# Stick-breaking heads: running sums as two short products of a high and a low part in place of one full fp32 product

## The chip, the cores and the metric

The kernel runs as one program on 1 core of one Trainium2 chip. The metric is the device time of one execution in microseconds (us); less is better. The values shown are medians over runs of the same program.

## The reference, cut to what matters

The reference is a chain of transformer blocks on 256 tokens of width 1024, all in fp32. The change touches one piece of it, the attention of heads 0 to 7 in the first layer of the second block. Each of these heads is 64 wide and is called a stick-breaking head:

```python
strict = kpos[None, :] < qpos[:, None]
z = jnp.einsum('bhqd,bhkd->bhqk', q_blk, k).astype(jnp.float32) * scale
log_keep = jnp.where(strict, jax.nn.log_sigmoid(-z), 0.0)
suffix = lax.cumsum(log_keep, axis=3, reverse=True)
between = jnp.concatenate([suffix[..., 1:], jnp.zeros_like(suffix[..., :1])], axis=-1)
weight = jnp.where(strict, jnp.exp(jax.nn.log_sigmoid(z) + between), 0.0)
return jnp.einsum('bhqk,bhkd->bhqd', weight.astype(v.dtype), v)
```

The other heads of that layer are softmax heads, and everything around them (projections, output matrix, gated feed-forward parts) is dense matrix products with weights streamed from memory.

## The kernel before, in words

**Weights.** All weight matrices are packed into 231 pieces of 128 x 2048 fp32 (1 MB each). A piece is loaded by a DMA of the sync queue into one of three `raw` buffers, ScalarE (ACT) casts it to `hi` (fp32r, the high part, L2359), VectorE (DVE) subtracts to get `lo` (raw minus hi, L2685), and TensorE (PE) then makes three fp32r products, hi*hi, hi*lo and lo*hi. There are three `hi` and three `lo` buffers, so the cast of piece i+3 waits until TensorE has used piece i.

**Order.** Every engine runs one list of instructions in order. The list, `script`, is made on the host by a planner. `emit(kind, pe=..., act=..., dve=...)` appends a step and adds its estimated costs to each engine's due time. In the attention stage `weave` runs many generators side by side: the two tracks that split weight pieces, the tracks of the query and key norms, a filler (`projections`, which makes the query, key and value products and then the product with `w_out_2`), and a pool of up to PAIRS = 4 head pairs. At each turn it takes the generator whose next engine comes free first; a generator that yields None is stuck until something else has been emitted. So a changed cost or an added step can change the order of all that follows in the stage. The parts of the first attention layer are made in the order Q1, K1, Q0, V0, K0, V1 (0 and 1 are halves of 512 columns), then `w_out_2`, whose k-th block of rows needs the output of pair k.

**A stick-breaking pair.** Pairs m = 0 to 3 are stick-breaking, two heads each (`sticks`), pairs 4 to 7 are softmax pairs (`softmaxes`), and pair m + 4 starts when pair m is over. The steps of a stick pair are: `sb_z` on TensorE (scores, L2280); `sb_log` on ScalarE (two copies out of PSUM L2611, then Abs L2614, Exp L2616, Ln L2618); `sb_keep` on VectorE (L3128, and the two triangular masks L3130 and L3131); `sb_sum` on TensorE (the running sums, L2290 to L2292); `sb_add` on VectorE (L3136); `sb_exp` on ScalarE (L2622); `sb_mask` on VectorE (L3140, L3141); then `pv`, the product with the values, on TensorE (L2328), and the split of its result (`o_hi` L2638, `o_lo` L3162). The scores of a head lie in a tile of 384 columns: 256 queries against the first 128 keys, and the last 128 queries against the last 128 keys. Softmax pairs have `soft` (L2308), `soft_top`, `soft_exp` (L2627, L2629), `soft_div`, `soft_turn` (transposes, L2317), `turn_out` (L2635) and `pv`. The query and key evacuation ahead of `sb_z` is L3050.

**The running sum before.** The tile `Eb[i]` (fp32, both heads of a pair) is the moving operand; the stationary operand is `ntri`, minus the triangle of ones, or `nones`, minus all ones, both fp32 constants. For each head there is one product of 256 columns and two of 128 columns. The `nt` buffers hold a norm's turned rows, and `fgb` is a buffer that the second attention layer uses for its forget gate.

## Time and profile before

| what | value |
|---|---|
| median of 3 runs | 1449.74 us (1448.24 to 1449.86) |
| span of the profiled execution | 1447.7 us |
| TensorE busy | 1434.0 us, 99% |
| TensorE weight loads busy | 1233.0 us, 85% |
| VectorE busy | 1013.2 us, 70% |
| ScalarE busy | 769.4 us, 53% |
| GpSimd busy | 29.4 us, 2% |

The profiled execution has no time of its own on record apart from its span, which runs from its first to its last instruction. The median of the runs is 2.0 us above that span; that is what lies around it, start and end, and the scatter of runs. Busy times overlap between engines. A matrix product appears as a weight load (PEld) and a matmul (PE); the ends of matmuls are modelled and overlap, so the distance between starts is the measure of their cost.

### The profile page before, as it was taken

The numbers are of one execution on the slowest core, as the hardware profiler recorded it, in microseconds if no ns is written. First come the engines' busy times: TensorE is split into PE (matmuls) and PEld (weight loads), VectorE is DVE, ScalarE is ACT, GpSimd is POOL, SyncE is SP. The second block draws the span as 40 slices with busy tenths as digits, with TensorE's granted clock in tenths as the row PEclk, the third lists the DMA queues.
The fourth block names the chain that finished last, engine by engine and source line by source line (L and its number), as shares of the span: only waits on it lengthen the run. The fifth ranks groups of instructions, "written<-read, shape, count | busy, mean of one in ns | idle before, by whom it ended". The sixth has DMA issues, their size and how long they took to land.

```text
span 1447.7 us, 22866 instructions
## 1 busy us (share of the span) xinstructions
PE 1434.0 (99%) x9408; PEld 1233.0 (85%) x9408; DVE 1013.2 (70%) x1341; ACT 769.4 (53%) x1047; POOL 29.4 (2%) x96
## 2 busy tenths in 40 slices
PE   9999999999999999999999999999999999999999
PEld 8988898888887888888878888888888887788887
DVE  6876567886356787548768877478774688687753
ACT  7744564654336565445665554355553556665542
POOL 0000000000001200000000000000000000000000
PEclk9999999999999999999999999999999999999999
DMA  8431235555544455544424555545555453255552
GB/s 337 169 119 63 87 117 204 198 202 203 190 159 175 156 220 179 202 174 180 170 88 157 193 199 182 201 158 205 190 189 191 152 196 123 94 207 188 190 188 87
DMA packets 36104, 249.11 MB, mean 172 GB/s; under 512 B 4129, under 2 KB 4257, under 8 KB 6689
## 3 DMA queue, kind: packets, MB, share of 16 engines
q1 hardware_dynamic: 35712, 247.46, 47.2%
q8 instruction: 75, 1.23, 0.3%
q10 hardware_dynamic: 288, 0.19, 0.0%
q14 instruction: 29, 0.23, 0.0%
HBM read 246.59 MB, written 1.05 MB: 171 GB/s over the span
## 4 chain that ended last, share of the span: by engine, by line
PE 66%; DVE 1%; issue 0%; POOL 0%; ACT 0%; DVEq 0%; ACTq 0%; POOLq 0%
PE ps L1995 20%; PE ps L2002 10%; PE ps L1910 10%; PE ps L1912 10%; PE ps L1911 10%; PE ps L1985 2%; PE ps L1984 1%; PE ps L2328 1%; PE ps L2308 1%; PE ps L2052 1%; PE ps L2317 0%; PE ps L2256 0%; DVE lo L2685 0%; PE ps L1981 0%; PE ps L2290 0%
## 5 line engine op out<-in xcount | busy, mean ns | idle before, releaser
L2685 DVE TENSOR_TENSOR lo<-raw,hi 128x2048 fp32r<-128x2048 f32 (+1 forms) x230 | 525.3, 2285 | 226.7 <-ACT hi L2359 226.5
L2359 ACT CAST hi<-raw 128x2048 fp32r<-128x2048 f32 (+1 forms) x230 | 438.0, 1905 | 249.0 <-PE ps L1912 245.2
L1995 PE MATMUL ps<-h,hi 128*128 128x512 f32 x1472 | 351.5, 390 | 0.0
L1995 PEld LDWEIGHTS ps<-h,hi 128*128 128x128 f32 x1472 | 270.5, 188 | 51.3
L1910 PE MATMUL ps<-hi,a 128*128 128x512 f32 x584 | 230.2, 394 | 0.0
L1912 PE MATMUL ps<-hi,a 128*128 128x512 f32 x584 | 227.6, 390 | 0.0
L1911 PE MATMUL ps<-lo,a 128*128 128x512 f32 x584 | 227.3, 389 | 0.0
L2002 PEld LDWEIGHTS ps<-h,lo 128*128 128x128 f32 x1472 | 188.1, 190 | 7.7
L2002 PE MATMUL ps<-h,lo 128*128 128x256 f32 x1472 | 190.3, 282 | 0.0
L2548 ACT COPY a<-ps 128x256 f32<-128x256 f32 x208 | 76.3, 372 | 203.7 <-PE ps L1995 100.9
L1910 PEld LDWEIGHTS ps<-hi,a 128*128 128x128 f32 x584 | 109.6, 188 | 24.1 <-issue 2.0
L1912 PEld LDWEIGHTS ps<-hi,a 128*128 128x128 f32 x584 | 109.6, 188 | 23.2
L1911 PEld LDWEIGHTS ps<-lo,a 128*128 128x128 f32 x584 | 109.7, 188 | 21.8
L2678 DVE TENSOR_TENSOR a<-ps,a 128x256 f32<-128x256 f32 x208 | 85.2, 422 | 32.4 <-ACT a L2548 30.7
L1910 PE MATMUL ps<-h,hi 128*128 128x256 f32 x352 | 104.1, 296 | 0.9 <-DVE lo L2685 0.9
L1911 PE MATMUL ps<-h,hi 128*128 128x256 f32 x352 | 99.5, 283 | 0.0
L1912 PE MATMUL ps<-h,lo 128*128 128x256 f32 x352 | 99.4, 282 | 0.0
L1910 PE MATMUL ps<-hi,h 128*128 128x512 f32 x208 | 84.5, 406 | 0.0
L1912 PE MATMUL ps<-hi,h 128*128 128x512 f32 x208 | 81.3, 391 | 0.0
L1911 PE MATMUL ps<-lo,h 128*128 128x512 f32 x208 | 81.2, 390 | 0.0
L1910 PEld LDWEIGHTS ps<-h,hi 128*128 128x128 f32 x352 | 67.2, 191 | 4.1 <-DVE lo L2685 1.1
L1911 PEld LDWEIGHTS ps<-h,hi 128*128 128x128 f32 x352 | 67.3, 191 | 0.2
(347 smaller groups left out, 1595.9 us busy)
## 6 DMA issues: line engine op xcount, KB each, us to landing
raw<-ws SPq DMA_DIRECT2D x229, 1024.0 KB, 4.8
X<-xin SPq DMA_DIRECT2D x8, 256.0 KB, 5.3
raw<-ws SPq DMA_DIRECT2D x2, 512.0 KB, 6.3
out<-X SPq DMA_DIRECT2D x4, 256.0 KB, 2.1
small<-small SPq DMA_DIRECT2D x1, 992.5 KB, 12.6
const<-const SPq DMA_DIRECT2D x1, 900.0 KB, 6.6
a<-row SPq DMA_DIRECT2D x1, 512.0 KB, 7.0
const<-const SPq DMA_DIRECT2D x1, 388.0 KB, 13.1
```

The costliest lines, as they stand in the source:

```text
L1910: e.matmul(o, ah, bh, start=start, stop=False)
L1911: e.matmul(o, ah, bl, start=False, stop=False)
L1912: return e.matmul(o, al, bh, start=False, stop=stop)
L1984: e.matmul(b2(sl)[:, 0, :], wl[:, k, a:a + 128], HH[:, k, :], start=False, stop=False)
L1985: t = e.matmul(b2(sl), wh[:, k, a:a + 128], h2[:, k, :, :], start=False, stop=k == 7)
L1995: t = e.matmul(b2(s["slots"][u]), wh[:, k, 128 * u:128 * u + 128], h2[:, k, :, :], start=k == 0, stop=last)
L2002: t = e.matmul(b2(s["slots"][u])[:, 0, :], wl[:, k, 128 * u:128 * u + 128], HH[:, k, :], start=False, stop=last)
L2052: t = e.transpose(banks[sl.b][:, 128 * u:128 * u + 128], X[:, s["b"], c:c + 128], ident)
L2359: e.copy(hi[j % NSPL][:, n], raw[j % NRAW][:, n]).then_inc(hi_ready, 1)
L2548: e.copy(half_to[s["to"]][s["j"]][:, s["u"], :], b2(sl)[:, 1, :]).then_inc(half_a.sem, 1)
L2678: e.tensor_tensor(to[:, u, :], b2(x)[:, 0, :], half_to[kind][j][:, u, :], ALU.add).then_inc(free[x.b], 1)
L2685: e.tensor_tensor(lo[j % NSPL][:, n], raw[j % NRAW][:, n], hi[j % NSPL][:, n].bitcast(F), ALU.subtract).then_inc(lo_ready, 1)
```

## The change

The running sums are made from fp32r operands. ScalarE casts `Eb` to a high part `EH` (a new step `sb_hi`), VectorE subtracts it from `Eb` in place to leave the low part `EL` (a new step `sb_low`; `EL[i]` lies on `Eb[i]`), and TensorE makes each of the three products twice, once with each part, adding in PSUM. The triangle and the all-ones matrix are copied once to fp32r tiles that lie in `fgb` (a new step `sb_tri`). There is only one `EH`, laid over the `nt` buffers, so a pair may write it only when the pair before has made its sums: the planner holds a pair back while `state["sticks"]` is "busy", and ScalarE waits for the bank of the sums before. The planner's cost of `sb_sum` goes from 2.2 to 1.1, and 0.75 (ScalarE) and 0.85 (VectorE) are added.

```diff
+        nt0 = top[0]
...
+        eb0 = ta.here() - 2 * PAIRS * 4 * 768
+        EL = [Arena(eb0 + 4 * 768 * i)([128, 2, 384], R) for i in range(PAIRS)]
+        EH = at("stick_hi", [128, 2, 384], R, nt0)
+        ntri, nones = fgb[:, 0:128], fgb[:, 128:256]
...
+                while state.get("sticks") == "busy":
+                    yield None
+                before, state["sticks"] = state.get("sticks"), "busy"
+                yield "act"
+                emit("sb_hi", act=0.75, i=i, v=keep_v, v_a=head_a.add(), before=before)
+                hi_v = head_a.n
+                yield "dve"
+                emit("sb_low", dve=0.85, i=i, v_a=hi_v, v=head_v.add())
+                low_v = head_v.n
                 yield "pe"
                 yield from room(3)
                 c = [take(), take()]
-                emit("sb_sum", pe=2.2, slots=c, i=i, v=keep_v)
+                emit("sb_sum", pe=1.1, slots=c, i=i, v=low_v)
+                state["sticks"] = c[1]
...
+            else:
+                emit("sb_tri", v_a=head_a.add())
...
                 elif kind == "sb_sum":
                     e.wait_ge(head_v.sem, s["v"])
-                    e.wait_ge(tables_in, 16)
                     for p, c in enumerate(s["slots"]):
                         claim(c)
-                        o, E = banks[c.b], Eb[s["i"]][:, p, :]
-                        e.matmul(o[:, 0:256], K("ntri"), E[:, 0:256], start=True, stop=False)
-                        e.matmul(o[:, 128:256], K("nones"), E[:, 256:384], start=False, stop=True)
-                        e.matmul(o[:, 256:384], K("ntri"), E[:, 256:384], start=True, stop=True).then_inc(full[c.b], 1)
+                        o = banks[c.b]
+                        parts = EH[:, p, :], EL[s["i"]][:, p, :]
+                        for n, E in enumerate(parts):
+                            e.matmul(o[:, 0:256], ntri, E[:, 0:256], start=n == 0, stop=False)
+                        for n, E in enumerate(parts):
+                            e.matmul(o[:, 128:256], nones, E[:, 256:384], start=False, stop=n == 1)
+                        for n, E in enumerate(parts):
+                            t = e.matmul(o[:, 256:384], ntri, E[:, 256:384], start=n == 0, stop=n == 1)
+                        t.then_inc(full[c.b], 1)
...
+                elif kind == "sb_tri":
+                    e.wait_ge(tables_in, 16)
+                    e.copy(ntri, K("ntri"))
+                    e.copy(nones, K("nones")).then_inc(head_a.sem, 1)
+                elif kind == "sb_hi":
+                    e.wait_ge(head_v.sem, s["v"])
+                    if s["before"]:
+                        ready(s["before"])
+                    e.copy(EH[:, :, :], Eb[s["i"]][:, :, :]).then_inc(head_a.sem, 1)
...
+                elif kind == "sb_low":
+                    e.wait_ge(head_a.sem, s["v_a"])
+                    e.tensor_tensor(EL[s["i"]][:, :, :], Eb[s["i"]][:, :, :], EH[:, :, :].bitcast(F),
+                                    ALU.subtract).then_inc(head_v.sem, 1)
```

## Rows read from the trace of the kernel before

**Rows 1.** The page, part 1: busy time, share and instructions of each engine.

```profile
PE 1434.0 (99%) x9408; PEld 1233.0 (85%) x9408; DVE 1013.2 (70%) x1341; ACT 769.4 (53%) x1047; POOL 29.4 (2%) x96
```

**Rows 2.** Waits of the PE engine over the whole span, one of them.

```profile
PE ps L2280 <- DVE a L3050: 1.8, 2, 0.9
```

**Rows 3.** Stretches: length, busy us PE, PEld, DVE, ACT, POOL; PEclk, DMA share, GB/s.

```profile
714.40:718.00 3.60, 3.60 (x27) 3.37 (x25) 3.56 (x5) 3.44 (x7) 0.00 (x0) 1.00 0.14 18
718.00:721.40 3.40, 3.40 (x17) 2.84 (x17) 2.41 (x5) 3.24 (x6) 0.00 (x0) 1.00 0.74 294
721.40:725.40 4.00, 3.96 (x27) 3.40 (x26) 3.76 (x9) 1.65 (x3) 0.00 (x0) 1.00 0.00 0
725.40:740.40 15.00, 15.00 (x104) 10.87 (x104) 13.70 (x60) 10.72 (x32) 0.00 (x0) 1.00 0.01 2
```

**Rows 4.** Timeline of PE, second head's sums: start, duration, instruction, count.

```profile
715.40 0.60 PE L2290 MATMUL ps<-a,const 128*128 128x256 f32 x2
715.84 0.38 PE L2291 MATMUL ps<-a,const 128*128 128x128 f32 x2
716.06 0.39 PE L2292 MATMUL ps<-a,const 128*128 128x128 f32 x2
716.28 0.60 PE L2290 MATMUL ps<-a,const 128*128 128x256 f32 x2
```

**Rows 5.** Timeline of PE: the filler between the sums, later sums, the first pv.

```profile
717.96 0.48 PE L1910 MATMUL ps<-hi,h 128*128 128x512 f32 x1
718.27 0.40 PE L1911 MATMUL ps<-lo,h 128*128 128x512 f32 x1
718.51 0.39 PE L1912 MATMUL ps<-hi,h 128*128 128x512 f32 x1
...
721.23 0.40 PE L1912 MATMUL ps<-hi,h 128*128 128x512 f32 x1
...
723.42 0.70 PE L2290 MATMUL ps<-a,const 128*128 128x256 f32 x2
...
725.37 1.52 PE L2328 MATMUL ps<-a,a 128*64 128x256 f32 x16
```

**Rows 6.** Timeline: two neighbouring fp32r products of 256 columns.

```profile
710.80 0.28 PE L1910 MATMUL ps<-h,hi 128*128 128x256 f32 x1
...
710.92 0.28 PE L1911 MATMUL ps<-h,hi 128*128 128x256 f32 x1
```

**Rows 7.** Weight loads by form, 700 to 730 us; then six transposes on the timeline.

```profile
L1911 PEld LDWEIGHTS ps<-h,hi 128*128 128x128 f32 x26 | 5.0, 191 | 0.0
...
L2328 PEld LDWEIGHTS ps<-a,a 128*64 128x64 f32 x24 | 1.5, 136 | 0.9 <-issue 0.4
...
737.72 0.82 PE L2317 MATMUL ps<-const,a 128*128 128x128 f32 x6
```

**Rows 8.** Groups by form, 690 to 800 us: busy time, mean ns, idle before.

```profile
L2685 DVE TENSOR_TENSOR lo<-raw,hi 128x2048 fp32r<-128x2048 f32 x15 | 34.3, 2287 | 9.0 <-ACT hi L2359 9.0
L2359 ACT CAST hi<-raw 128x2048 fp32r<-128x2048 f32 x15 | 28.6, 1906 | 10.4 <-PE ps L1912 10.4
...
L3128 DVE SCALAR_TENSOR_TENSOR a<-a,a 128x768 f32<-128x768 f32 x4 | 3.8, 957 | 2.4 <-ACT a L2618 2.4
...
L2369 ACT CAST h<-nt 128x512 fp32r<-128x512 f32 x4 | 2.5, 621 | 9.4 <-DVE nt L2710 9.4
```

**Rows 9.** Timeline of ACT from the piece cast to the stick pairs' exponentials.

```profile
712.62 1.88 ACT L2359 CAST hi<-raw 128x2048 fp32r<-128x2048 f32 x1
...
720.64 0.94 ACT L2618 ACTIVATE a<-a,const 128x768 f32<-128x768 f32 x1
```

**Rows 10.** Timeline of PE at the end of the stage's heads.

```profile
751.18 0.87 PE L2317 MATMUL ps<-const,a 128*128 128x128 f32 x6
...
753.68 0.87 PE L2328 MATMUL ps<-a,a 128*64 128x256 f32 x8
```

**Rows 11.** Timeline of ACT before the stage: the gap that sb_tri falls into.

```profile
655.52 0.62 ACT L2369 CAST h<-nt 128x512 fp32r<-128x512 f32 x1 [1.32 <-DVE nt L2710]
```

## The prediction

> **What bounds the kernel now.** I read the page first. TensorE is busy 99% of the span, VectorE 70%, ScalarE 53% [rows 1], so whatever shortens TensorE's list can show in the end time, and whatever makes TensorE wait costs its full length. The second view was the list of who waited for whom on TensorE: it waited very little anywhere, and in the stage of the change only 1.8 us, twice 0.9, where `sb_z` follows straight on the evacuation of the last key columns [rows 2]. The third view was the busy time by stretch. From 714.4 to 740.4 us, in which the stick pairs' sums and what hangs on them lie, TensorE is busy practically throughout at a granted clock of 1.00 (the 2.4 GHz level), while ScalarE is filled to 3.44 of 3.60 and 3.24 of 3.40 us up to 721.4, and VectorE to 3.56 of 3.60, 3.76 of 4.00 and 13.70 of 15.00 us [rows 3]. So the stage is bound by TensorE, and the two engines that get the new work are close to full exactly there. The last view was the timeline, for prices and order.
>
> **The sums on TensorE: removed.** A head's three fp32 products show as six records. From the start of one head's sums to the next is 716.28 - 715.40 = 0.88 us: 0.44 for the 256 columns and 0.22 for each 128 [rows 4]. Eight heads are 8 x 0.88 = 7.04 us.
>
> **Added.** Six fp32r products for each head, two of 256 columns and four of 128. A 256-column fp32r product costs 710.92 - 710.80 = 0.12 us from start to start [rows 6]; two are 0.24. A fp32r product of 128 columns does not occur in this trace, so I bound it. Below: 128 columns at 2.4 GHz are 0.053 us; with the 0.013 that the 256-column product has over its 0.107, that is 0.067, and a head costs 0.24 + 4 x 0.067 = 0.51. Above: the short form gets no fast rate and costs what the fp32 product of 128 columns costs, 0.22 [rows 4], and a head costs 0.24 + 0.88 = 1.12. Between them lies a bound by weights. Every product here brings its own load of 128 columns. A load of 128 columns is 191 ns long and one of 64 columns 136 ns [rows 7], so 64 columns more cost 55 ns and 128 columns some 110: this part cannot shrink with the moving columns. Six transposes of 128 columns also stand about 0.11 us apart ((0.82 - 0.27)/5, with 0.27 for the last one's tail as the time by which the record outlasts its start) [rows 7]. I take 0.12, the spacing of the product nearest in kind. Then a head costs 6 x 0.12 = 0.72, and the sums 5.76 in place of 7.04: **1.3 us less**. The ends are 8 x (0.88 - 0.51) = 3.0 us less and 8 x (1.12 - 0.88) = 1.9 us more.
>
> The rows say 0.11 to 0.12 for anything with a fresh load of 128 columns. The Trainium skill, page "TensorE: Matmul & The Clock Gate", section "LDWEIGHTS (loading the stationary operand)", gives a load as its columns divided by 1.2 GHz, 107 ns here, which agrees with the 110 from the rows. Its section "Back-to-back issue gap" however gives about 81 ns for a product of 128 columns in a stream of loads and products; by it a head would be an estimated 0.24 + 0.32 = 0.56 us and the gain 2.5 us. No run here shows such a product, and I keep to the row.
>
> **Change of form.** After fp32 sums the first fp32r product of the filler takes 718.27 - 717.96 = 0.31 us to the next start, where the steady distance is (721.23 - 718.51)/12 = 0.227 [rows 5]. That is 0.08 us at each return, and with all-fp32r sums it may go. For four or so places I take 0.3 us, with 0 as the other end. The same could fall away at the entry into the sums, which I leave out.
>
> **ScalarE: added.** Four casts of 128x768. By the casts of 512 and 2048 columns, 0.621 and 1.906 [rows 8], one is 0.621 + 256 x 1.285/1536 = 0.84 us, 3.3 us together. They lie where ScalarE is full [rows 3]. The two copies of `sb_tri` are smaller than the 0.62 cast [rows 8], and their step stands ahead of the cast at 655.52, before which ScalarE was idle for 1.32 us [rows 11]. I cost them at nothing; the cover is that gap, and without it the next norm's parts would be at most 1.2 us later, with TensorE's filler products in front.
>
> **VectorE: added.** Four subtractions of 128x768, by L3128 of that size 0.96 us each [rows 8], 3.8 us together, also where VectorE is nearly full.
>
> **What this does to the order.** The four pairs' sums are now a chain. A pair's cast waits for its own `sb_keep` and for the sums of the pair before, then comes the subtraction, then the sums: 0.84 + 0.96 + 2 x 0.72 = 3.24 us and three handovers of about 0.1, so 3.5 us for each pair at best. Behind the waiting cast on ScalarE stand the next pairs' `sb_log` steps (714.41 to 721.48 for two pairs, the end of the second Ln [rows 9]) and the piece casts of 1.9 us. VectorE's `lo`, `sb_keep` and `sb_add` steps stand behind the waiting subtraction. In the kernel before, the first two pairs' sums stood back to back from 714.4 to 717.96 and the other two were over at 725.37, when `pv` begins [rows 3, 5]. Now the first pair's subtraction can begin only behind the second pair's `sb_keep`, at about 714.5, and its sums come at about 715.6. The second pair's cast then meets ScalarE in the logs of pairs 2 and 3, and may come only behind both, about 722.5. Following the planner's rule I get the last sums between 727.5 (four turns without queues) and about 732, so 2 to 7 us later than before.
>
> Does that make TensorE wait? It has cover: two V1 pieces, 48 products at 0.227 = 10.9 us, were ready, and before they were spread up to 740 between the heads' work. From 714.4 to about 730, when the outputs of pairs 0 and 1 should be split and `w_out_2` may begin, I count 10.9 for V1, three pairs' sums 4.3, two `pv` at half of 1.52 each [rows 5] 1.5, and two `soft` and one `soft_turn` of some 0.8 each 2.3: 19 us of work for 16 us. At the far end, the last pair's transposes and its `pv` stand at 751.18 and 753.68 [rows 10], placed close before `w_out_2` needs them; a pair that comes a few us later still fits between. So the delay should be hidden for the most part. Some is not: each sum is a new handover VectorE to TensorE that the planner times by estimates, and the two such places that the trace shows cost 0.9 each [rows 2]. For four of them I take 0.2 each on average, 0.8 us, between 0 and 3.6.
>
> **Sum.** -1.3 - 0.3 + 0.8 = -0.8 us. On the profiled span that is 1447.7 - 0.8 = 1446.9; the median of the runs stands 2.0 above that span, so I forecast 1449.74 - 0.8 = **1448.9 us**.
>
> **The rivals.**
>
> *A. The short products are as fast as their columns.* For it: nothing in the trace shows that a load can't be faster under a short product, and the PE records of 256 columns stand no farther apart than 107 ns plus 13. Against it: the spacing of the loads [rows 7]. -3.0 - 0.3 + 0.8 = -2.5: 1447.2 us. With no new waits, 1446.4.
>
> *B. The short products run at the fp32 rate.* For it: the kernel has no fp32r product under 256 columns, so no row excludes it. Against it: the rate of fp32 comes with two records for each product, and fp32r shows one. +1.9 - 0.3 + 0.8 = +2.4: 1452.1 us, inside the band of no change but at its edge.
>
> *C. The chain of the four pairs leaves TensorE dry: slower.* The place is ScalarE's list after 715 us: if the second pair's cast stands behind both logs, and the later ones each behind a piece cast that itself waits for TensorE, pairs 2 and 3 reach `pv` after V1 is used up, and `w_out_2` cannot begin its second piece. For it: ScalarE and VectorE are full there [rows 3], and a piece cast waits for TensorE's use of an older piece in the same list. Against it: 19 us of work for 16. It decides once the second pair's output comes 3 us later than I have it; past that each us costs one us. With 4 to 5 us dry, -1.6 + 4.5 gives 1452.6, and up to 1454.
>
> *D. Only the chain's place changes.* The gain and the new waits cancel: 1449.7. I count it with the forecast.
>
> **How the numbers follow.** A measurement of this kernel can tell some 0.2% (2.9 us) from no change, that is below 1446.8 or above 1452.6. Forecast with D 0.55 (its own range 1447.6 to 1450.4), A 0.17, B 0.13, C 0.15. Faster: half of A and a little of the forecast's tail, 0.12. Slower: nearly all of C and a third of B, 0.19. Same: 0.69. The range for 8 in 10 takes in A but for its extreme, B, and the nearer part of C: 1446.3 to 1453.3.
>
> **What would show it.** The starts of the sums' products: 0.12 apart for both sizes (0.067 or 0.22 for the short ones are A and B); a head 0.72 from the next. Casts of 128x768 of 0.84 us, subtractions of 0.96. The last sums at 727 to 732. The list of TensorE's waits: new rows for the sums behind the subtraction, together under 1 us; rival C would show as waits of more than 2 us in one place between 725 and 745, on a value product or on `w_out_2`. The `sb_tri` copies at about 654 with nothing waiting for them. The prediction is wrong if the planner reorders weight pieces such that a piece's `lo` comes late, which I could follow only.

## The result and the profile after

The changed kernel is slower: 1454.91 us, median of 4 runs (1453.85 to 1455.73), against 1449.8 us for the kernel before beside it (1448.24 to 1450.1). The ratio is 1.0038, with a 95% interval of 1.0023 to 1.0052. The profiled execution took 1454.62 us around a span of 1452.8 us. The forecast was 1448.9, in a range of 1446.3 to 1453.3, so the result is slower than the whole range. The runs of the kernel before lie near 1448.2 or near 1449.9 us (the part on the clock below shows why), and three of the four here are of the upper kind; beside the later medians of 1448.4 to 1448.7 the changed kernel is 6.2 to 6.5 us slower.

The page, part 1, of the kernel after, beside [rows 1]:

```profile
PE 1434.8 (99%) x9408; PEld 1233.5 (85%) x9408; DVE 1017.2 (70%) x1345; ACT 773.3 (53%) x1053; POOL 29.5 (2%) x96
```

The page hardly moves. VectorE and ScalarE each gained 4 us of busy time, which is the new work; TensorE's share is 99% in both. What grew is the span. The waits of TensorE over the whole span of the kernel after (beside [rows 2]; the line of the wait, what it waited for, us in all, times, longest) say more:

```profile
PE ps L2308 <- DVE a L3164: 2.7, 1, 2.7
...
PE ps L2297 <- DVE a L3080: 1.8, 2, 0.9
...
PE ps L2338 <- DVE a L3196: 0.6, 1, 0.6
```

The row of 1.8 is the one of [rows 2] under a new line number. The row of 2.7 is new and the longest wait in the list: the sums (L2308) waited once for the subtraction (L3164). Stretches of the kernel after, read as [rows 3]:

```profile
725.40:728.00 2.60, 2.60 (x24) 2.25 (x22) 1.56 (x2) 1.80 (x2) 0.00 (x0) 1.00 0.00 0
728.00:731.00 3.00, 0.34 (x7) 0.11 (x1) 3.00 (x5) 3.00 (x5) 0.00 (x0) 1.00 0.29 68
731.00:734.00 3.00, 3.00 (x13) 2.87 (x14) 3.00 (x4) 1.09 (x2) 0.00 (x0) 0.52 0.68 284
734.00:737.00 3.00, 3.00 (x15) 1.55 (x16) 1.94 (x4) 0.81 (x3) 0.00 (x0) 0.50 0.92 325
737.00:740.40 3.40, 3.40 (x22) 2.56 (x21) 2.48 (x13) 1.19 (x4) 0.00 (x0) 0.86 0.07 27
```

Three things are to be seen here. From 728 to 731 TensorE is busy for 0.34 of 3.00 us while VectorE and ScalarE are both busy for all of it: TensorE is dry because of them. Then the granted clock falls from 1.00 to 0.52 and 0.50, the 1.2 GHz level, and is back at 1.00 only in the last stretch. And up to 728 nothing is wrong.

**The products.** TensorE's timeline in the kernel after, the first pair's sums (beside [rows 4]):

```profile
716.44 0.28 PE L2308 MATMUL ps<-stick_hi,a 128*128 128x256 f32 x1
716.55 0.28 PE L2308 MATMUL ps<-a,a 128*128 128x256 f32 x1
716.67 0.22 PE L2310 MATMUL ps<-stick_hi,a 128*128 128x128 f32 x1
716.73 0.28 PE L2310 MATMUL ps<-a,a 128*128 128x128 f32 x1
716.84 0.28 PE L2312 MATMUL ps<-stick_hi,a 128*128 128x128 f32 x1
...
717.06 0.33 PE L2308 MATMUL ps<-stick_hi,a 128*128 128x256 f32 x1
717.24 0.28 PE L2308 MATMUL ps<-a,a 128*128 128x256 f32 x1
...
717.75 0.44 PE L1927 MATMUL ps<-hi,h 128*128 128x512 f32 x1
718.03 0.39 PE L1928 MATMUL ps<-lo,h 128*128 128x512 f32 x1
```

The first head takes 717.06 - 716.44 = 0.62 us, the second 717.75 - 717.06 = 0.69, the pair 1.31. Four pairs are 5.24 us where they were 7.04: the products alone save 1.8 us. The starts are not even: 0.06 after the first of the `nones` products, 0.18 after the first product of the second head, 0.11 or 0.12 elsewhere. The weight loads of the first head's products, on the timeline of the kernel after, are more even:

```profile
716.56 0.19 PEld L2310 LDWEIGHTS ps<-stick_hi,a 128*128 128x128 f32 x1
716.67 0.19 PEld L2310 LDWEIGHTS ps<-a,a 128*128 128x128 f32 x1
```

From the second on, the loads start 0.11 to 0.12 us apart, one for each product, and so do the products in the mean, long or short: 1.31/12 = 0.109. The first `nones` product starts 0.11 behind its load, with the 256 columns ahead of it, and the next one 0.06 behind its own. The 0.18 in the second head these rows do not explain.

**The place of the wait.** TensorE's timeline in the kernel after, from the second pair's outputs on (in brackets the idle time and what ended it):

```profile
727.36 0.87 PE L2349 MATMUL ps<-a,a 128*64 128x256 f32 x8
730.90 0.42 PE L2308 MATMUL ps<-stick_hi,a 128*128 128x256 f32 x1 [2.67 <-DVE a L3164]
...
733.53 0.76 PE L1927 MATMUL ps<-hi,a 128*128 128x512 f32 x1
...
738.07 0.50 PE L1927 MATMUL ps<-hi,a 128*128 128x512 f32 x1
...
739.56 0.28 PE L2308 MATMUL ps<-stick_hi,a 128*128 128x256 f32 x1
```

At 727.36 `pv` of pair 0 is made, and then there is nothing else on TensorE's list before the sums of pair 2. ScalarE's timeline of the kernel after, in the same time:

```profile
721.39 0.82 ACT L2648 CAST stick_hi<-a 128x768 fp32r<-128x768 f32 x1
723.50 0.69 ACT L2615 ACTIVATE a<-ps,st 128x512 f32<-128x512 f32 x1 [1.29 <-PE ps L1929]
724.09 0.83 ACT L2652 ACTIVATE a<-a 128x768 f32<-128x768 f32 x1
724.82 1.90 ACT L2380 CAST hi<-raw 128x2048 fp32r<-128x2048 f32 x1
727.52 0.83 ACT L2648 CAST stick_hi<-a 128x768 fp32r<-128x768 f32 x1 [0.80 <-PE ps L2312]
```

VectorE's timeline of the kernel after:

```profile
723.19 0.95 DVE L3164 TENSOR_TENSOR a<-a,stick_hi 128x768 fp32r<-128x768 f32 x1
...
726.75 2.29 DVE L2715 TENSOR_TENSOR lo<-raw,hi 128x2048 fp32r<-128x2048 f32 x1 [1.03 <-ACT hi L2380]
728.96 1.01 DVE L3170 TENSOR_TENSOR a<-a,ps 128x384 f32<-128x384 f32 x2
729.89 0.95 DVE L3164 TENSOR_TENSOR a<-a,stick_hi 128x768 fp32r<-128x768 f32 x1
```

Read backwards from TensorE's start at 730.90: the subtraction of pair 2 ran at 729.89. Its operand, the cast of 727.52, was over at 728.35, so it was not the cast that it waited for but its turn on VectorE, behind the `sb_add` of pair 1 (728.96) and the weight piece's `lo` (726.75, 2.29 us). That `lo` had itself waited 1.03 us for the piece cast at 724.82, which stood on ScalarE behind the exponential of pair 0 (724.09), behind the value evacuation (L2615), which had idled 1.29 us until TensorE finished the value product of its bank. The second pair's low part, on the other hand, was ready at 724.14, and its sums came only at 725.96, since the V1 products stood ahead of them. So TensorE used up its filler (all of V1) before pair 1's sums, and had none left when it waited for pair 2's.

**Where the 5 us are.** I measure the stage from the start of the second `sb_z` (712.92 before, 712.08 after) to the first transposes of the next norm (763.23 and 768.06): 50.31 us before, 55.98 after, 5.7 more. The sums give 1.8 back. The wait is 2.67. At the lower clock pair 2's sums take 733.53 - 730.90 = 2.63 us to the next start where pair 1's take 727.36 - 725.96 = 1.40 (1.2 more). What follows up to 738.07 (three products, one `pv`, eight `soft` products) takes 4.54, where the same pieces take 0.90 (755.01 to 755.91), 0.80 (740.97 to 741.77) and 0.85 (741.77 to 742.62) at full clock, 2.55 together (2.0 more): 3.2 for the clock. -1.8 + 2.7 + 3.2 = 4.1. Of the other 1.6 us, 0.9 is in two smaller waits, 0.60 at 751.12 and 0.32 at 748.79; 0.7 I have not traced. The spans differ by 5.1 us and not by 5.7 or more, since the profile of the kernel before lost 1.6 us to the clock ahead of the stage, which that of the kernel after did not (see the part on the clock).

### The profile page after: what moved, and what is told of

The parts are those of the page before. It is cut to its first block, busy times and chain, and to the rows that moved or that the text cites. A ratio compares the mean times of both kernels' runs of the same rounds, so it can differ in the third digit from the quotient of the medians.

```text
span 1452.8 us, 22879 instructions
## 1 busy us (share of the span) xinstructions
PE 1434.8 (99%) x9408; PEld 1233.5 (85%) x9408; DVE 1017.2 (70%) x1345; ACT 773.3 (53%) x1053; POOL 29.5 (2%) x96
## 4 chain that ended last, share of the span: by engine, by line
PE 65%; DVE 1%; ACT 1%; issue 1%; POOL 0%; DVEq 0%; ACTq 0%; POOLq 0%
PE ps L2012 20%; PE ps L2019 10%; PE ps L1927 10%; PE ps L1929 10%; PE ps L1928 10%; PE ps L2002 1%; DVE lo L2715 1%; PE ps L2001 1%; PE ps L2349 1%; PE ps L2329 1%; PE ps L2069 1%; ACT hi L2380 0%; PE ps L2338 0%; PE ps L2273 0%; PE ps L1998 0%
```

## The experiments

All kernels ran beside the kernel before, whose median was 1448.4 to 1448.7 us. "Planned" is the planner's cost of `sb_sum`. "Stage" is the length just defined, in the profiled execution, which need not be a typical one: for cast_once it was the fastest run (1451.61 us), for high_only the slowest (1447.22), and for cast_pool22 one of the slower ones (1451.04). Most kernels were timed at different times, and their medians are compared all the same, so a difference under some 2 us between two kernels is not firm unless their runs or profiles are named beside it.

| kernel | planned | median us | ratio (95%) | stage us |
|---|---|---|---|---|
| own_high | 1.1 | 1455.49 | 1.0046 (1.0034 to 1.0059) | 57.24 |
| two_high | 1.1 | 1455.25 | 1.0045 (1.0033 to 1.0058) | 57.24 |
| after_warm | 1.1 | 1453.22 | 1.0035 (1.0023 to 1.0047) | 54.85 |
| after_warm10 | 1.1 | 1452.73 | 1.0032 (1.0019 to 1.0045) | 54.26 |
| after_true | 1.3 | 1455.21 | 1.0046 (1.0034 to 1.0059) | 56.04 |
| own_true | 1.3 | 1455.47 | 1.0046 (1.0033 to 1.0059) | 57.26 |
| cast_once | 1.3 | 1454.50 | 1.0035 (1.0022 to 1.0047) | 53.60 |
| after_moved | 1.1 | 1455.51 | 1.0050 (1.0037 to 1.0064) | 56.96 |
| split_only | 2.2 | 1451.05 | 1.0015 (1.0006 to 1.0023) | 52.71 |
| own_order22 | 2.2 | 1450.68 | 1.0018 (1.0009 to 1.0026) | 52.18 |
| after_22 | 2.2 | 1449.62 | 1.0008 (0.9999 to 1.0017) | 50.86 |
| products_only | 2.2 | 1449.66 | 1.0007 (0.9998 to 1.0017) | 51.43 |
| prod_replan | 1.3 | 1447.95 | 0.9994 (0.9985 to 1.0003) | 49.91 |
| pool_split | 1.3 | 1449.67 | 1.0005 (0.9996 to 1.0013) | 51.32 |
| cast_pool | 1.3 | 1448.07 | 0.9999 (0.9990 to 1.0007) | 49.71 |
| cast_pool22 | 2.2 | 1449.42 | 1.0009 (1.0000 to 1.0018) | 50.83 |
| high_only | 0.7 | 1445.68 | 0.9980 (0.9971 to 0.9989) | 47.80 |
| before_11 | 1.1 | 1449.02 | 1.0004 (0.9996 to 1.0013) | 50.92 |

### Is it the one high tile and its hold? own_high and two_high

The first theory after the result was that the single `EH` serializes the pairs. own_high gives each pair a tile of its own and drops the hold and the wait; two_high lets two tiles take turns.

```diff
-        EH = at("stick_hi", [128, 2, 384], R, nt0)
+        EH = [Arena(40 * 1024 + 4096 * i)([128, 2, 384], R) for i in range(PAIRS)]
...
-                while state.get("sticks") == "busy":
-                    yield None
-                before, state["sticks"] = state.get("sticks"), "busy"
+                before = None
```

> Theory 1 (the single high tile, and the hold on the pairs that it needs, makes the loss): each pair has a high tile of its own and no pair waits for the sums of the one before. Pair 2's sums are ready before V1 is used up, TensorE has no wait of more than 0.5 us at the sums and its clock stays at 1.00; the time falls from 1454.9 to 1447.5 to 1449.5 us. Theory 2 (casts and subtractions overfill ScalarE and VectorE, whatever the hold): the sums are still late, the wait at the sums stays above 1.5 us, and the time stays at 1453 us or more.

> Two high tiles in turn: a pair waits for the sums of the pair two before. Theory 1: pair 2's cast needs only pair 0's sums, over at 717.8 us, so the long wait goes; pair 3 still waits for pair 1. Time 1448 to 1451 us. Theory 2: no change beyond 1 us from 1454.9.

Measured: 1455.49 (1454.39 to 1456.0) and 1455.25. Nothing came back. A wait of TensorE in own_high:

```profile
PE ps L2305 <- DVE a L3161: 2.7, 1, 2.7
```

The same wait of 2.7 us is there with four tiles, because the casts were late in their own right: those of pairs 2 and 3 stand on ScalarE behind a piece cast at 724.19, and start at 725.98. The granted clock was 0.61 and 0.50 in 730 to 735 and 735 to 740. The hold on the tile is not the cause.

### The parts one by one: products_only, prod_replan, high_only, split_only

products_only keeps the order of the kernel before and makes only the six fp32r products. `sb_keep` writes a rounded tile, which is used twice, so there is no cast and no subtraction. prod_replan is the same, planned with 1.3.

```diff
-                        o, E = banks[c.b], Eb[s["i"]][:, p, :]
-                        e.matmul(o[:, 0:256], K("ntri"), E[:, 0:256], start=True, stop=False)
...
+                        parts = EL[s["i"]][:, p, :], EL[s["i"]][:, p, :]
+                        for n, E in enumerate(parts):
+                            e.matmul(o[:, 0:256], ntri, E[:, 0:256], start=n == 0, stop=False)
...
```

> The kernel before in its own order, with six fp32r products for each head, both times of the rounded tile that the masks write; the subtraction that makes the low part, and the cast, are left out, so the sums are those of the rounded values, twice. By the trace of the changed kernel a pair's sums take 1.31 us in place of 1.77: 1.8 us less, so about 1448.0 us (1447 to 1449). If the products were themselves at fault (rival), the time would be that of before or more.

> The products alone (the low part and the cast left out, sums of the rounded tile twice), with the planner's cost of the sums at 1.3 in place of 2.2. If the gain of 1.8 us was lost because the order was made for slower sums, the wait of 1.25 us before pair 2's or 3's sums goes, the clock stays at 1.00, and the time is 1446.5 to 1447.5. If pairs 2 and 3 are simply paced by ScalarE's logs, TensorE waits 1 us or more again somewhere, with the fall of the clock, and the time is 1448.5 to 1450.

Measured: 1449.66 (1447.79 to 1451.62) and 1447.95 (1447.49 to 1449.97), both above the range that I had expected for a gain kept whole. In the old order the saving went into a wait. The wait of TensorE in products_only, and then two stretches:

```profile
PE ps L2297 <- DVE a L3146: 1.2, 1, 1.2
```

```profile
720.00:725.00 5.00, 3.75 (x26) 3.43 (x26) 4.27 (x10) 2.38 (x4) 0.00 (x0) 0.82 0.01 2
725.00:730.00 5.00, 5.00 (x43) 3.39 (x39) 3.63 (x12) 2.35 (x5) 0.00 (x0) 0.84 0.00 0
```

The shorter sums reach pair 3's `sb_keep` (L3146) 1.25 us too early; that step is paced by ScalarE's logs, so 1.2 of the 1.8 us turn into idle time. The clock then falls for a while too (0.82 and 0.84). The spread of this kernel is the clock: the run with a mean of 1.0 took 1447.79, that with 0.997 took 1451.62. With the plan redone (prod_replan) the wait and the fall are gone, and the kernel is some 0.7 us faster than before by its medians, which the interval does not tell from nothing.

high_only goes a step further down: one rounded tile, three products, planned with 0.7. It leaves the low part out of the running sums.

> The high part alone: the masks write the tile rounded to fp32r, three products for each head, no cast and no subtraction, sums planned at 0.7. It leaves the low part out of the running sums. TensorE has 7.04 - 8 x 0.33 = 4.4 us less work than before. If ScalarE's logs pace pairs 2 and 3, part of that comes back as waits and I expect 1446 to 1448; if the planner fills the place, 1444.5; if the clock falls, 1449.

Measured: 1445.68 (1445.16 to 1447.22), the only kernel that is faster beyond its interval. So TensorE's time in this stage does count when nothing else is added. A pair's sums take 0.74 us there (714.81 to 715.55) where they took 1.76, 4.1 us less for the four, of which some 2.8 arrived.

split_only is the other half of the change: a high tile for each pair, cast and subtraction are made and waited for, but the sums are the fp32 products of the high part alone, so the low part is left out.

```diff
-                        parts = EH[s["i"]][:, p, :], EL[s["i"]][:, p, :]
...
+                        o, E = banks[c.b], EH[s["i"]][:, p, :].bitcast(F)
+                        e.matmul(o[:, 0:256], K("ntri"), E[:, 0:256], start=True, stop=False)
...
```

> The cast and the subtraction without the new products: each pair has its own high tile, the sums are the three fp32 products again (of the high part alone, the low part is made and waited for but left out of the sums), planned at 2.2. Split theory: the added steps alone make the wait, at 2 us or more, and the fall of the clock, so 1453 to 1456. If it takes both the steps and the shorter sums, the longer sums fill the wait: 1450 to 1452.

Measured: 1451.05 (1450.57 to 1451.64) at a granted clock of 1.0, with no wait of TensorE over 0.9 us in the stage. The two new steps in the chain cost 2.4 us here; in the stage TensorE is idle for 2.2 us (52.71 less 50.48 busy) where it was idle for 0.3, so most of it is in small waits. Products and split alone, +1.2 and +2.4 or less, do not add up to the 5 to 7 us of the full change. That the rest lies in the order was the next theory.

### Is it the clock? after_warm and after_warm10

The kernel after, with 20 (or 10) products on unused data put on TensorE just before pair 2's wait. Their results are not used. For this the claims of the sums' banks move ahead of the wait for the low part, in all four pairs.

```diff
+                    for c in s["slots"]:
+                        claim(c)
+                    if s["i"] in (2,):
+                        for _ in range(20):
+                            e.matmul(banks[s["slots"][0].b][:, 0:256], ntri, HH[:, 0, :], start=True, stop=True)
                     e.wait_ge(head_v.sem, s["v"])
...
-                        claim(c)
```

> The changed kernel, with 20 products of 256 columns on data that nobody uses, into the bank of pair 2's sums ahead of the wait for its low part (2.4 us at 0.12). The wait of 2.7 us stays in length, but TensorE works through it. If the fall of the clock is a cost of its own: granted clock 1.00 from 725 to 740 us, and 3.3 us less than 1454.9, about 1451.6. If the clock is only a sign and costs nothing here: 1454.9.

> The changed kernel with 10 products on unused data in place of 20 ahead of pair 2's wait. With 20 they began late, when the bank was free, and ran 1.3 us past the moment at which the low part was ready, so part of the gain of the clock was given back. With 10 (1.2 us) I expect the clock at 1.00 and a time 1 us under that with 20: about 1452. If 10 are too few to hold the clock, 1454 to 1455.

Measured: 1453.22 (1452.85 to 1455.46) and 1452.73 (1452.04 to 1454.22), 1.7 and 2.2 us below the kernel after (1453.85 to 1455.73, so the ranges overlap), with a granted clock of 1.00 in every stretch from 715 to 740. The timeline of TensorE in after_warm:

```profile
729.05 2.63 PE L2306 MATMUL ps<-h,a 128*128 128x256 f32 x20 [1.43 <-DVE a L3174]
```

The added products waited 1.43 us themselves for their bank and ended 1.2 us after the sums could have started, which is why less came back than expected. The profiled executions, whose clock ahead of the stage was 1.00 in all three kernels, compare cleanly: 1454.62 for the kernel after, 1452.86 and 1452.59 with the products. What is shown: with the wait filled, the clock does not fall, and about 2 us of the loss go with that.

The clock falls in another place too, outside the stage. Every kernel of this study waits 1.8 to 1.9 us at about 480 us, before the transposes of a norm (L2058 before, L2075 after). TensorE's timeline in the kernel before, then a stretch of it, then the timeline in the kernel after:

```profile
482.04 0.68 PE L2058 MATMUL ps<-nt,const 128*128 128x128 f32 x4 [1.85 <-DVE nt L2721]
...
489.69 3.79 PE L1995 MATMUL ps<-h,hi 128*128 128x512 f32 x16
```

```profile
483.00:485.00 2.00, 2.00 (x9) 1.71 (x8) 1.97 (x2) 0.00 (x0) 0.00 (x0) 0.50 0.69 283
```

```profile
482.75 0.68 PE L2075 MATMUL ps<-nt,const 128*128 128x128 f32 x4 [1.77 <-DVE nt L2751]
...
488.84 3.79 PE L2012 MATMUL ps<-h,hi 128*128 128x512 f32 x16
```

The same products take 489.69 - 482.04 = 7.65 us behind a clock of 0.50, and 488.84 - 482.75 = 6.09 at 1.00: 1.6 us more after nearly the same wait. Five of the 20 profiled executions show this fall (before, after_true, pool_split, high_only, cast_pool22), the others do not. That is the distance between the two kinds of runs of the kernel before: near 1448.2 at a mean clock of 1.000, near 1449.9 at 0.999. Behind the wait of 2.67 us in the stage, on the other hand, the clock fell in all five profiles that have it (after, own_high, two_high, after_true, own_true).

The five runs of cast_once (next part) took 1451.61 us at a mean clock of 0.999, 1453.54 at 0.998, and 1454.5, 1455.26 and 1456.08 at 0.996. A mean that is 0.003 lower over 1450 us is 8.7 us at half the clock, in which 4.4 us of work are lost; 1456.08 - 1451.61 = 4.5. So the spread of this kernel is the clock. The mean does not say where it fell; up to 1.6 us can be the place at 480 us. So a wait costs its length and, where the clock falls behind it, 1.6 to 3.2 us more: in five of 20 profiles behind the wait of 1.8 us, in five of five behind that of 2.67.

### Is it the planner's numbers? after_true, own_true, cast_once, before_11

The planned 1.1, 0.75 and 0.85 are lower than the 1.31, 0.83 and 0.95 that the trace shows. after_true plans the kernel after, own_true the kernel own_high, with measured costs.

```diff
-                emit("sb_hi", act=0.75, i=i, v=keep_v, v_a=head_a.add(), before=before)
+                emit("sb_hi", act=0.84, i=i, v=keep_v, v_a=head_a.add(), before=before)
...
-                emit("sb_sum", pe=1.1, slots=c, i=i, v=low_v)
+                emit("sb_sum", pe=1.3, slots=c, i=i, v=low_v)
```

> The changed kernel with one edit in the plan: the costs of the new steps as measured (sums 1.3, cast 0.84, subtraction 0.96 in place of 1.1, 0.75, 0.85). If the loss comes from an order made with too low costs, which uses up the filler ahead of pair 1's sums, some filler stays for the place before pair 2's sums, the clock holds, and the time is 1449.5 to 1452. If the single high tile (the hold) makes the loss once the order is right, 1453.5 or more.

> A high tile for each pair with the measured costs in the plan. Beside the one tile with the same costs this tells what the hold costs: by my reading nothing over 1 us. Time 1449.5 to 1452 if too low costs made the loss; 1454 to 1456 if only an overstated cost of 2.2 helps, by chance of the order.

Measured: 1455.21 and 1455.47, as without it, and after_true has the same wait of 2.7 us. True costs don't mend the order, and both came out above the range that I had expected if too low costs made the loss. cast_once has own tiles and appends the cast to ScalarE's list at once behind `sb_keep`, without a turn of its own.

```diff
-                yield "act"
                 emit("sb_hi", act=0.75, i=i, v=keep_v, v_a=head_a.add(), before=before)
...
-                emit("sb_sum", pe=1.1, slots=c, i=i, v=low_v)
+                emit("sb_sum", pe=1.3, slots=c, i=i, v=low_v)
```

> As the kernel with a high tile for each pair, but the planner appends a pair's cast to ScalarE's list at once when its keep step is planned, and counts the sums at 1.3. Pair 1's cast then stands ahead of pairs 2 and 3's logs, and the casts of pairs 2 and 3 ahead of the next piece cast. Place theory (the loss comes from where the casts stand in ScalarE's order, behind the logs and a piece cast): no wait over 1 us at the sums, no fall of the clock, time 1448 to 1450.5. Load theory (the added work on two full engines delays the heads wherever it stands): the heads come late all the same, a wait of 2 us or more stays, 1453 or more.

Measured: 1454.50 (1451.61 to 1456.08), again a miss for the place theory. The earlier cast only moved the idle time (3.8 us in two places before `pv`, 3.1 us of it in one). before_11 is the kernel before, planned with 1.1 and nothing else changed.

> The kernel before with one edit in the plan: the cost of its fp32 sums at 1.1 in place of 2.2. The instructions are the same, the order may differ. If a wrong planned cost alone costs time, 1450 or more; if the order only matters together with the later sums of the change, 1448 to 1449.

Measured: 1449.02 (1448.51 to 1450.26). The plan with 1.1 costs the old kernel half a microsecond by the medians, which the interval (0.9996 to 1.0013) does not tell from nothing.

### Is it the order? own_order22, after_22, after_moved

The smallest edit of the whole study: the changed kernel, with `sb_sum` planned at 2.2 as before the change, 0.9 us too high. No instruction is added or removed (the page counts 9408, 1345 and 1053 on TensorE, VectorE and ScalarE in both); only the order of the list differs, and with it the PSUM banks that the steps get. own_order22 does the same to own_high.

```diff
-                emit("sb_sum", pe=1.1, slots=c, i=i, v=low_v)
+                emit("sb_sum", pe=2.2, slots=c, i=i, v=low_v)
```

> The kernel with a high tile for each pair and all six products, its only edit the planner's cost of the sums at 2.2, as in the kernel with the split alone (1451.05 us). Both then have nearly the same order. If short products in an order made for long ones uncover TensorE, a wait of 2 us or more with a fall of the clock stands at the sums or behind them and the time is 1452 or more. If it was the cost of 1.1 in the plan that made the loss, the time is 1.8 us below the split alone, about 1449.3.

> The changed kernel with the old planned cost of 2.2 for the sums. With a high tile for each pair that edit took 1455.5 to 1450.7 us. If the hold costs nothing of its own, 1450 to 1451.5; if it does, 1452.5 or more, with a wait of over 1.5 us before pair 2's or pair 3's sums.

Measured: own_order22 1450.68 (1450.24 to 1452.07), 4.8 us below own_high; after_22 1449.62 (1449.0 to 1451.29), 5.3 us below the kernel after, at a granted clock of 1.0. The profiled executions, both at 1.00 ahead of the stage, give the same: 1454.62 and 1449.62, with stages of 55.98 and 50.86. The order was what cost, and the single tile with its hold costs nothing that shows here. ScalarE's timeline in after_22, to be laid beside that of the kernel after:

```profile
722.21 0.84 ACT L2652 ACTIVATE a<-a 128x768 f32<-128x768 f32 x1
722.96 1.90 ACT L2380 CAST hi<-raw 128x2048 fp32r<-128x2048 f32 x1
724.76 0.67 ACT L2615 ACTIVATE a<-ps,st 128x512 f32<-128x512 f32 x1
726.26 0.83 ACT L2648 CAST stick_hi<-a 128x768 fp32r<-128x768 f32 x1 [0.82 <-PE ps L2312]
```

VectorE's timeline in after_22:

```profile
724.89 2.29 DVE L2715 TENSOR_TENSOR lo<-raw,hi 128x2048 fp32r<-128x2048 f32 x1
727.12 0.96 DVE L3164 TENSOR_TENSOR a<-a,stick_hi 128x768 fp32r<-128x768 f32 x1
```

The exponential and the piece cast stand ahead of the value evacuation here, so ScalarE does not idle for 1.29 us, the piece's `lo` starts at 724.89 in place of 726.75, and the subtraction comes ahead of `sb_add`, at 727.12 in place of 729.89. On TensorE two value products (of three records each) are left between `pv` of pair 0 and pair 2's sums, which begin at 728.40 without an idle time.

Which of these differences carries it? after_moved tests the simplest: the kernel after, with the last four filler steps (12 products) taken from before pair 1's sums and put before pair 2's, on TensorE alone.

```diff
+        sums = [j for j, s in enumerate(script) if s["kind"] == "sb_sum"]
+        mine = [j for j in range(sums[1]) if script[j]["kind"] == "rows"][-4:]
+        taken = [script[j] for j in mine]
+        for j in reversed(mine):
+            del script[j]
+        script[sums[2] - 4:sums[2] - 4] = taken
```

> The changed kernel, plan and costs as they are, except that after planning the last four filler steps (12 products, 2.7 us) are moved in TensorE's order from before pair 1's sums to before pair 2's sums. Every other engine's order is the same. If the place of the filler makes the loss, the wait before pair 2's sums falls from 2.7 to about 1.2 us or less, the clock stays at 1.00, and the time is 1449.5 to 1451.5. If the loss lies in the work or in the single tile, 1453.5 or more.

Measured: 1455.51 (1455.3 to 1456.71), a miss. The timeline of TensorE in after_moved:

```profile
724.05 0.39 PE L2319 MATMUL ps<-stick_hi,a 128*128 128x256 f32 x1 [0.80 <-DVE a L3175]
730.73 0.38 PE L2319 MATMUL ps<-stick_hi,a 128*128 128x256 f32 x1 [1.26 <-DVE a L3175]
734.85 0.77 PE L1938 MATMUL ps<-hi,a 128*128 128x512 f32 x1 [2.54 <-DVE a L3207]
```

The one wait of 2.67 became three, 4.6 us together. Part of it was filled as meant (1.26 is left). But on ScalarE the value evacuation (L2626 here) now waited 2.29 us for the moved products, until 729.57, and the next piece cast stood behind it, at 730.16; its `lo` (732.08, 2.29 us) stood ahead of pair 0's `o_lo` on VectorE (734.29), and `w_out_2` waited for that. Filler on TensorE can't be shifted by itself; the lists of ScalarE and VectorE have to change with it. Which single step of them makes the difference in after_22 I have only argued from the traces, not tested.

### The new work on GpSimd: pool_split, cast_pool, cast_pool22

GpSimd is busy for 2% of the span. pool_split gives it cast and subtraction, cast_pool the cast alone; both have own tiles and are planned with 1.3, cast_pool22 with 2.2.

```diff
+                elif kind == "sb_pool":
+                    e.wait_ge(head_v.sem, s["v"])
+                    e.tensor_copy(EH[s["i"]][:, :, :], Eb[s["i"]][:, :, :]).then_inc(head_p.sem, 1)
+                    e.wait_ge(head_p.sem, s["h"])
+                    e.tensor_tensor(EL[s["i"]][:, :, :], Eb[s["i"]][:, :, :], EH[s["i"]][:, :, :].bitcast(F),
+                                    ALU.subtract).then_inc(head_p.sem, 1)
```

> The cast and the subtraction both on GpSimd, which is idle here, with a high tile for each pair and a planned 3.0 us for the two. ScalarE and VectorE are as full as before the change. If they were the trouble, the time is 1446.5 to 1449.5 even if GpSimd takes 1.5 us for each of the two; if the longer chain of a pair is itself the trouble, TensorE waits 1.5 us or more at the sums and the time is 1452 or more. How long GpSimd takes for 128x768 no row shows; above 3 us each the chain decides.

> Only the cast is on GpSimd (0.83 us there, by the trace of the kernel with both steps on it), the subtraction is back on VectorE, one high tile for each pair, sums planned at 1.3. With both steps on GpSimd its subtraction of 1.8 us stretched VectorE's instructions beside it (a piece's subtraction of 2.29 to 3.90). If that overlap was what remained, time 1447.5 to 1449.5 and no VectorE instruction over 2.5 us; if the 3.8 us of subtractions on VectorE delay the heads again, 1450 to 1453.

> The full-precision version that came out best, the cast on GpSimd and the subtraction on VectorE with a tile for each pair, with the planned cost of the sums at 2.2, since that order left filler ahead of the late sums. TensorE has 1.8 us less work than before and ScalarE no more than before; if no wait over 1 us is left, 1446.5 to 1448, under the kernel before; if VectorE's 3.8 us still delay the heads, 1448 to 1450.

Measured: 1449.67 (1448.86 to 1450.75), 1448.07 (1447.59 to 1449.96) and 1449.42 (1449.04 to 1451.48). cast_pool is the best version that keeps both parts: it takes 0.8 us x 4 off ScalarE, and comes out level with the kernel before. cast_pool22 missed the better of its two ranges, 1446.5 to 1448. No version with both parts beats the kernel before by more than its interval. Here the plan with 1.3 is the better one and that with 2.2 is worse by 1.3 us: no planned cost is good for all variants. The timeline of GpSimd in pool_split:

```profile
718.61 1.84 POOL L3235 TENSOR_TENSOR a<-a,a 128x768 fp32r<-128x768 f32 x1
722.13 0.83 POOL L3233 CAST a<-a 128x768 fp32r<-128x768 f32 x1 [1.68 <-DVE a L3157]
723.04 2.53 POOL L3235 TENSOR_TENSOR a<-a,a 128x768 fp32r<-128x768 f32 x1
...
727.29 1.88 POOL L3235 TENSOR_TENSOR a<-a,a 128x768 fp32r<-128x768 f32 x1
```

VectorE's timeline in pool_split, beside it:

```profile
718.85 2.42 DVE L3154 SCALAR_TENSOR_TENSOR a<-a,a 128x768 f32<-128x768 f32 x1
...
727.42 3.90 DVE L2711 TENSOR_TENSOR lo<-raw,hi 128x2048 fp32r<-128x2048 f32 x1
```

VectorE's steps that start inside a subtraction on GpSimd become longer: 2.42 for the 0.96 of L3128 and 3.90 for the 2.29 of `lo` [rows 8]. The GpSimd instruction of 718.61 ended at 720.45, and the VectorE instruction 0.82 us after that; that of 727.29 ended at 729.17, and the `lo` 2.15 us after that, in both cases about the instruction's own length. The Trainium skill, page "SBUF — State Buffer", section "SBUF: two separate sides", says that the two engines share a pair of ports which the first to start holds for its whole instruction while the other is blocked, where the VectorE step has two inputs in SBUF, as these two have; these rows agree. The GpSimd cast of 722.13, beside an addition of VectorE that reads PSUM (L3166, at 721.99), kept its 0.83 us.

## Why the prediction was wrong, step by step

**The step that failed** is the one that ends with "So the delay should be hidden for the most part." Its working set 19 us of work against 16 us of time, and treated the work as if it could be spent wherever it was needed. TensorE's list spent it otherwise: all of V1 stood ahead of pair 1's sums (up to 725.96), and nothing but one `pv` between them and pair 2's. The total was there, the place was not. Rival C, which had a chance of 0.15, is what happened: its mechanism (the chain of the pairs behind logs and piece casts), its sign, and nearly its place (a wait of more than 2 us in one place between 725 and 745, but on the sums themselves, not on a value product or `w_out_2`). C's price, 1452.6 and up to 1454, was still too low by 1 to 2 us, since it had the wait alone, at 4 to 5 us: 2.67 and the two smaller waits make 3.6, and the clock 3.2 more. No term of the sum, nor of a rival, had the granted clock falling after the wait, and that was as large as the wait: 3.2 us against 2.67 in the profiled execution. The trace of the kernel before had shown such a fall, 1.6 us after a wait of 1.85 at 482 us, outside the stretches that I read. The range ended at 1453.3 for the same reason.

**New handovers.** The term of 0.8 us, "between 0 and 3.6", measured 2.67 + 0.9 us of waits (and 0.7 us not traced). The bound from [rows 2] took two short waits as the measure for all; a chain behind a full engine is of another kind.

**The sums on TensorE.** 1.8 us less for a forecast of 1.3: right in kind, the size off by a third. The pair takes 1.31 us, not 1.44. The reason given, that the load of 128 columns sets the pace whatever the moving columns, fits the rows: the products are 0.109 apart in the mean and their loads 0.11. I should have taken that 0.11 of [rows 7] in place of the 0.12 of [rows 6]. Rival A (0.067) is out, and so is rival B (0.22). By the Trainium skill's 81 ns (page "TensorE: Matmul & The Clock Gate", section "Back-to-back issue gap") the gain was to be an estimated 2.5; these runs don't show that rate: 109 ns was measured.

**Change of form.** The first product after the sums still takes 718.03 - 717.75 = 0.28 us, where the steady distance is 0.227 and it was 0.31 before [rows 5]. So the 0.3 us of this term did not come; at most 0.03 a place did.

**The casts, subtractions and `sb_tri`.** 0.81 to 0.83 and 0.95 to 0.96 us for forecasts of 0.84 and 0.96; right. `sb_tri` shows as no wait of TensorE; the gap ahead of the cast [rows 11] took it.

**The order.** The pair 0 sums came at 716.44 (forecast about 715.6), the second cast behind both logs at 721.39 (about 722.5): the chain by hand was good up to there. The last sums came at 739.56, not by 727 to 732. From pair 1 on the hand count lacked the filler ahead of the sums and the wait itself.

**Rival D**, gain and waits cancel, is what most of the variants do, and the change itself does when it is planned with 2.2 (after_22). That the forecast and D had 0.55 was a fair view of the change, and a bad one of the particular order that the planner would make. The order turns on numbers that look harmless: the kernel after is 5.3 us faster planned with 2.2 than with 1.1, the kernel before about 0.5 (within its noise), and cast_pool is 1.3 us slower with 2.2 than with 1.3. The last sentence of the prediction named the risk (a piece's `lo` that comes late, which I could follow only), and it should have weighed more in the chances.

**Still open:** which one of the differences on ScalarE and VectorE between the orders planned with 1.1 and 2.2 carries the 5.3 us. after_moved shows only that the filler on TensorE isn't it by itself. Of the 1.6 us beside the large wait and the clock in the kernel after, 0.9 are two waits that were not tested one by one, and 0.7 have no cause yet. What decides whether the clock falls after a wait of 1.8 us is open too.

## What to carry to other kernels

Where a bottleneck engine lives on filler work, don't weigh the sum of the filler against the delay: see which filler still stands between the last handover and the next one in the list. When two added steps go onto the engines that feed the bottleneck, price the lists of those engines first; the gain on the bottleneck (1.8 us here) is small against one wait that it opens (2.7 and 3.2 for the clock). And where a planner makes the order, try a few planned costs before judging a change: the same instructions ran at 1454.9 and at 1449.6 us.

## What the runs showed of the hardware that was not expected

- A single idle time of TensorE of 2.67 us after long unbroken work was followed by 6 to 7 us at a granted clock of 0.50 (1.2 GHz) in the kernel after, and the clock fell behind it in the four other profiles that have it too. After one of 1.8 to 1.9 us, in every kernel at about 480 us, the clock fell in five of 20 profiles (0.50 in 483 to 485 before, 1.6 us lost) and stayed at 1.00 in the others. In products_only an idle time of 1.25 us stood beside stretches at 0.82 and 0.84.
- fp32r products of 128 and of 256 columns cost the same when each has a fresh load of 128 columns: 0.109 us a product, with loads 0.11 us apart. So splitting an fp32 product of 128 columns (0.22) in two fp32r products saves next to nothing, and that of 256 columns (0.44) saves half. In high_only three such products for each head took 0.74 us a pair, against 1.31 for six.
- GpSimd casts 128x768 from fp32 to fp32r in 0.83 us, as fast as ScalarE (0.82), beside an addition of VectorE that reads PSUM, and in 2.83 beside a `lo` of VectorE (at 715.71 in pool_split). Its subtraction of that size takes 1.8 to 2.5 us against VectorE's 0.95, and VectorE steps with two SBUF inputs that start meanwhile take longer (2.42 for 0.96, 3.90 for 2.29).
